# RWKV recurrence in a fused two-block kernel: the halves of a tile take turns in scores, outputs and state updates, and the states of a whole tile are multiplied in one matmul

## What is computed

```
def step(S, inp):
    r_t, w_t, k_t, v_t, a_t, b_t = inp
    sa = jnp.einsum("bhij,bhj->bhi", S, a_t)
    S = S * w_t[:, :, None, :] + sa[..., None] * b_t[:, :, None, :] + v_t[..., None] * k_t[:, :, None, :]
    y = jnp.einsum("bhij,bhj->bhi", S, r_t)
    return S, y
```

## Time and profile before

| | |
|---|---|
| median of 3 runs | 2230.68 us (2229.61 to 2230.72) |
| the profiled execution | 2232.73 us |
| its span in the profile | 2230.9 us |
| PE busy | 2089.2 us, 94% |
| DVE, ACT, POOL busy | 49%, 41%, 57% |
| mean granted PE clock | 0.962 of full speed |
| the recurrence's stretch | from about 349 to 663 us of the span |

### The profile page before, as it was taken

The page is one execution under the profiler, slowest core; times in us unless marked ns, Lnnn a source line. Parts: engine busy times, 40 slices in busy tenths (PEclk is TensorE's granted clock), DMA queues, the critical chain, the costliest instruction groups (busy, mean ns, idle before and its releaser), DMA issues.

```text
span 2230.9 us, 41267 instructions
## 1 busy us (share of the span) xinstructions
PE 2089.2 (94%) x16208; PEld 1966.6 (88%) x16208; DVE 1094.1 (49%) x1627; ACT 918.0 (41%) x1578; POOL 1278.2 (57%) x528
## 2 busy tenths in 40 slices
PE   7999898889989999999996799999998988999997
PEld 7999687878879999999895499999998877898997
DVE  5860866655555871684145467512172325324431
ACT  5333451010024434433444544444455554655552
POOL 6786350000016787788571178868675553676885
PEclk9999898999999999999997899999999998999999
DMA  6444330000014454445341045544345332343552
GB/s 261 183 173 151 114 125 27 1 1 1 1 48 161 170 183 175 157 167 186 132 151 38 20 170 175 192 163 176 144 170 191 131 114 87 139 163 142 188 189 76
DMA packets 40909, 292.06 MB, mean 131 GB/s; under 512 B 4432, under 2 KB 5712, under 8 KB 5712
## 3 DMA queue, kind: packets, MB, share of 16 engines
q1 hardware_dynamic: 40640, 289.18, 36.0%
q10 hardware_dynamic: 144, 1.05, 0.1%
HBM read 289.17 MB, written 1.05 MB: 130 GB/s over the span
## 4 chain that ended last, share of the span: by engine, by line
issue 31%; PE 30%; POOLq 18%; POOL 17%; ACT 1%; DVE 1%; DMA 0%; DVEq 0%; SPq 0%; ACTq 0%
POOLq L1827 17%; POOL w_low L1823 17%; PE ps L574 9%; PE ps L582 9%; PE ps L578 9%; PE ps L1219 1%; PE ps L1207 1%; PE ps L1197 1%; PE ps L686 0%; POOLq L1822 0%; DMA X<-x_in 0%; ACT units L1729 0%; ACT units L1284 0%; POOLq L1839 0%; DVE units L1849 0%
## 5 line engine op out<-in xcount | busy, mean ns | idle before, releaser
L1823 POOL TENSOR_TENSOR w_low<-wring,w_high 128x1024 fp32r<-128x1024 f32 x524 | 1278.0, 2454 | 931.5 <-ACT w_high L1284 902.9
L574 PE MATMUL ps<-in_high,w_high 128*128 128x256 f32 (+1 forms) x2856 | 832.2, 291 | 33.7 <-DVE in_low L1849 12.9
L582 PE MATMUL ps<-in_high,w_low 128*128 128x256 f32 (+1 forms) x2856 | 822.7, 288 | 0.0
L578 PE MATMUL ps<-in_low,w_high 128*128 128x256 f32 (+1 forms) x2856 | 820.9, 287 | 0.0
L1284 ACT ACTIVATE w_high<-wring 128x1024 fp32r<-128x1024 f32 x524 | 542.1, 1055 | 289.2 <-PE ps L574 284.8
L574 PEld LDWEIGHTS ps<-in_high,w_high 128*128 128x128 f32 x2856 | 547.7, 192 | 43.2 <-issue 37.6
L578 PEld LDWEIGHTS ps<-in_low,w_high 128*128 128x128 f32 x2856 | 547.4, 192 | 0.4
L582 PEld LDWEIGHTS ps<-in_high,w_low 128*128 128x128 f32 x2856 | 547.8, 192 | 0.0
L574 PE MATMUL ps<-hid_high,w_high 128*128 128x272 f32 (+1 forms) x880 | 255.0, 290 | 0.0
L582 PE MATMUL ps<-hid_high,w_low 128*128 128x272 f32 (+1 forms) x880 | 250.8, 285 | 0.0
L578 PE MATMUL ps<-hid_low,w_high 128*128 128x272 f32 (+1 forms) x880 | 250.6, 285 | 0.0
(11 more groups left out here) (310 smaller groups left out, 2762.1 us busy)
## 6 DMA issues: line engine op xcount, KB each, us to landing
wring<-stream SPq DMA_DIRECT2D x271, 1024.0 KB, 4.8
con<-consts SPq DMA_DIRECT2D x1, 2455.0 KB, 16.4
X<-x_in SPq DMA_DIRECT2D x1, 1088.0 KB, 7.4
units<-decay ACTq DMA_DIRECT2D x1, 1024.0 KB, 4.7
out<-AL SPq DMA_DIRECT2D x1, 1024.0 KB, 4.7
par<-params SPq DMA_DIRECT2D x1, 187.0 KB, 4.9
con<-consts SPq DMA_DIRECT2D x1, 130.0 KB, 7.3
```

Of the source, the lines that this page charges most:

```text
L574: mm = pe.matmul(o, wh, high(k), start=(k == 0), stop=False)
L578: mm = pe.matmul(o, wh, low(k), start=False, stop=False)
L582: mm = pe.matmul(o, wl, high(k), start=False, stop=(k == kt - 1))
L1823: pool.tensor_tensor(w_low[:, (half + h) % SPLIT_RING, :], wring[:, slot, h * HALF * P:(h + 1) * HALF * P], w_high[:, (half + h) % SPLIT_R ...
```

## The change

The list of heads has `u` in the outer loop, so halves take turns. `rk_update` and `rk_output` are rewritten to issue each kind of matmul for both halves before the next kind. `rk_right` multiplies the states of both halves in one matmul of 128 columns, ahead of the two others; in chunk 0, which has no state, it only has the new order.

```diff
-            rk_heads = [(2 * par + u, par, u, HD * par) for par in range(2) for u in range(2)]
+
+            rk_heads = [(2 * par + u, par, u, HD * par) for u in range(2) for par in range(2)]
...
+                z = ps[0:C, 5, 0:4 * HD].rearrange("p (a u v) -> p u a v", a=2, u=2)
                 for q, par, u, p in rk_heads:
-                    o = ps[0:C, 5, q * HD:(q + 1) * HD]
-                    mm = pe.matmul(o, rk_lk[g % 2][c][0:C, q, 0, :], rk_tm[g % 2][c][0:C, 4 + u, p:p + HD],
-                                   start=True, stop=(c == 0))
-                    if c:
-                        mm = pe.matmul(o, T0[:, 2 * g + u, t0:t0 + C], rk_s[:, c - 1, u, par, :],
-                                       start=False, stop=True)
+                    if c and par == 0:
+                        pe.matmul(z[:, u, :, :], T0[:, 2 * g + u, t0:t0 + C], rk_s[:, c - 1, u, :, :],
+                                  start=True, stop=False)
+                    mm = pe.matmul(z[:, u, par, :], rk_lk[g % 2][c][0:C, q, 0, :], rk_tm[g % 2][c][0:C, 4 + u, p:p + HD],
+                                   start=(c == 0), stop=(c == 0 or par == 1))
                 mm.then_inc(S["rk_z_ready"], 1)
...
-                for q, par, u, p in rk_heads:
-                    o = ps[p:p + HD, rk_chain_banks(g)[0], u * HD:(u + 1) * HD]
-                    pe.matmul(o, tm[0:C, u, p:p + HD], rk_sa[0:C, q, :], start=True, stop=False)
-                    mm = pe.matmul(o, tm[0:C, 2 + u, p:p + HD], tm[0:C, 4 + u, p:p + HD], start=False, stop=True)
+                for u in range(2):
+                    pair = [(2 * par + u, HD * par, ps[HD * par:HD * (par + 1), rk_chain_banks(g)[0], u * HD:(u + 1) * HD])
+                            for par in range(2)]
+                    for q, p, o in pair:
+                        pe.matmul(o, tm[0:C, u, p:p + HD], rk_sa[0:C, q, :], start=True, stop=False)
+                    for q, p, o in pair:
+                        mm = pe.matmul(o, tm[0:C, 2 + u, p:p + HD], tm[0:C, 4 + u, p:p + HD], start=False, stop=True)
                 mm.then_inc(S["rk_s_ready"], 1)
...
-                for q, par, u, p in rk_heads:
-                    o = ps[p:p + HD, rk_chain_banks(g)[1], u * P:u * P + C]
-                    pe.matmul(o, rk_sa[0:C, q, :], lb[0:C, q, 1, :], start=True, stop=False)
-                    mm = pe.matmul(o, tm[0:C, 4 + u, p:p + HD], lk[0:C, q, 1, :], start=False, stop=(c == 0))
-                    if c:
+                for u in range(2):
+                    pair = [(2 * par + u, par, HD * par, ps[HD * par:HD * (par + 1), rk_chain_banks(g)[1], u * P:u * P + C])
+                            for par in range(2)]
+                    for q, par, p, o in pair:
+                        pe.matmul(o, rk_sa[0:C, q, :], lb[0:C, q, 1, :], start=True, stop=False)
+                    for q, par, p, o in pair:
+                        mm = pe.matmul(o, tm[0:C, 4 + u, p:p + HD], lk[0:C, q, 1, :], start=False, stop=(c == 0))
+                    for q, par, p, o in pair if c else ():
                         mm = pe.matmul(o, rk_s[p:p + HD, c - 1, u, par, :], A[p:p + HD, 2 * g + u, now],
                                        start=False, stop=True)
                 mm.then_inc(S["rk_y_ready"], 1)
```

## The result

| | before | after |
|---|---|---|
| median | 2230.7 us (4 runs, 2229.6 to 2231.0) | **2202.0 us** (4 runs, 2199.2 to 2203.3) |
| ratio, 95% interval | | **0.9871** (0.9853 to 0.9888) |
| the profiled execution, its span | 2232.73, 2230.9 us | 2199.24, 2197.4 us |
| mean granted PE clock in it | 0.962 | 0.968 |

Faster by 28.7 us.

The account below looks back on a forecast made before the run. PE bounds the recurrence, DVE following closely. 15.0 + 1.0 + 1.2 + 1.6 + 3.6 = 22.4 us of PE time, less 1.4 for margins, gives 21 less: 2230.68 - 21 = 2209.7 us, range 2205 to 2218.

Parts of the forecast that it names:

- outputs (chunks 1, 2 and 0): Recurrence outputs: 8 in chunks 1 and 2 fall from 3.76 to 1.88 us, saving 15.0; chunk 0 saves 1.0.
- state updates: Recurrence state updates: second half starts at once, saving 1.2 us in chunk 1 and 1.6 us in chunk 0.
- right sides: Chunks 1 and 2: joined matmul costs what one part did, two of eight go, 0.45 us in 8 places, 3.6 us.
- scores, logits: Scores and NSA logits: alternating them gains nothing, since their halves overlap already; 24 of each costed at nothing.
- Two halves share the array: Outputs: both halves run each kind of matmul together, so two heads take about the 0.94 us of one.
- The bank of line 838: Rival, 12%: line 838's pairs, sharing one PSUM bank, go one after the other; 3.4 us back, 2213.
- The column halves: Rival, 4%: column halves don't overlap in outputs moving 128 columns; only 5.7 us gained, 2225.
- DVE takes over: Rival, 10%: DVE sets the recurrence's pace and half the gain turns into waits, 2220.
- The 1.4 us that I took off for margins: Allowance for thin DVE margins at chunk 1's outputs and the very end, taking 22.4 us down to 21.
- Slower by a price per turn: Rival, 4%: each turn between halves in updates and outputs empties the array, 0.14 us each; 13.4 us slower, 2244.
- The price of a change of tile shape: Outputs of chunks 1 and 2: each change between 128 x 64 and 64 x 64 tiles costs some 0.14 us.
- after the recurrence everything is moved up as a whole: Behind the recurrence: later work only starts earlier, its weights already waiting; `rk_o` would begin near 642 instead of 663.00 us.

Follow-up runs that it names:

- the outputs alone: Kernel before with only the outputs taking the halves in turn: 2223.5 us, ratio 0.9950 (0.9933 to 0.9967).
- the updates alone: Kernel before with only the state updates taking the halves in turn: 2240.4 us, ratio 1.0010 (0.9989 to 1.0031).

## Why the prediction was right in its steps and wrong in its number

Array time of the steps in the whole recurrence, added up from each step's start to the start of the next matmul, before and after, in the first profile of either kernel and in the second:

| step | forecast | first profiles | second profiles |
|---|---|---|---|
| outputs (chunks 1, 2 and 0) | 15.0 + 1.0 | 33.7 to 18.4, **15.3** | 34.2 to 18.2, **16.1** |
| state updates | 1.2 + 1.6 | 8.1 to 5.3, **2.8** | 7.7 to 4.8, **2.9** |
| right sides | 3.6 | 16.7 to 14.4, **2.3** | 17.1 to 13.2, **3.9** |
| the three together | 22.4 | 58.4 to 38.0, **20.4** | 59.0 to 36.1, **22.9** |
| scores, logits | 0 | 0.007 each, 0.3 in all | |

Some of these steps fell on the lower clock; the right sides of the first changed profile hold one of 2.61 us at 613 us, where the others take 1.36 to 1.39. At the full clock a right side gives 0.45, eight of them 3.6.

- **Two halves share the array** at 128 columns as at 64: right, and with it the outputs.
- **Scores and logits are worth nothing**: right, as the change of their order alone showed. They are the first part of the diff to catch the eye, and their halves ran side by side already.
- **The bank of line 838**: right to take nothing. The Trainium skill (TensorEngine Tiling (Array Packing), Gotcha 1: PSUM Pressure), by which different row tiles cannot access one bank simultaneously, would have spread 845 out; the row with four records in the time of two does not show it, for two tiles at different rows and different columns whose outputs lie on different partitions.
- **The column halves**: the rival by the rule on row groups of the Trainium skill (TensorE: Matmul & The Clock Gate, Packing small matmuls) fell; the four records of 841 have 0.24 to 0.26 us over the same 128 rows, and without changes of shape those of 841 and 843 have 0.22.
- **DVE takes over**: didn't happen. The waits before the solves are 10.6 us in both, and the margin of the earlier trace rows was met exactly. The 1.4 us that I took off for margins were lost nowhere.
- **Slower by a price per turn**: fell. With no change of shape in between, rows of four records over two halves stand 0.22 us apart, the pace of one half alone.
- **The price of a change of tile shape**, 0.14 us: right, and it was the larger part of the matter: of the 1.85 us that an output lost, its removal alone gave 1.39 in the old order. In the changed kernel 0.56 of the 1.85 are four changes fewer and the rest is overlap; without any change of shape an output takes 1.46.

**The step that failed** is the last one: "after the recurrence everything is moved up as a whole", and with it "on the median's footing 2230.68 - 21". I took the clock as a property of the kernel: the clocks of the earlier trace rows entered only as a lower bound for the saved records, by which a cut at low clock is worth 4 to 5 us more. What the runs showed in its place is that parts with equal instructions were not moved up as a whole, 10.6 us of the 33.5 in the first profiles coming after `rk_o` had begun. The granted clock varies from one execution to the next, for the same kernel by 0.958 to 0.966, which goes with 2245 to 2227 us, and the changed kernel as it stands is nearly always granted more (0.966 or more in 10 of 12 executions; the kernel before in 8 of 83). At equal mean clock, 0.966, the kernel before has 2226.7 us and the changed one about 2203.8 (5 executions): 23 less, the sum of the steps with nothing taken off. The comparison isn't clean, as a shorter phase at the lower clock is itself what a higher mean is made of; that is why it is offered as the better reading and not as a proof. The rest of the measured 28.7 to 31.6 us, 6 to 9, is by this reading clock. The 1.4 us taken off for margins are a small second part of the miss.

That `rk_o` began 22.9 us earlier, so near to the sum, was in part luck: the steps gave 20.4 us in these two profiles, and the recurrence had 41.5 us at the lower clock instead of 47.0. Over more profiles it can be told apart. From the instruction at 301.4 us to `rk_o` five profiles of kernels with the old steps have 364.2 us on the mean, 50 of them at the lower clock, and seven with the whole change 337.3 and 38: 26.9 less. Among these seven the time goes from 334.1 us with 30.0 at the lower clock to 340.4 with 44.9, 0.42 us for each microsecond. By that the 12.5 us fewer are worth 5.3 and the steps 21.6 (an estimate), as summed. Behind the recurrence the surplus lies in the first attention and at the end of the sparse attention, which takes one of three lengths (as before, some 3.5 or 5 us less) in changed and unchanged kernels alike.

The range failed for the same reason: it was made of doubts about steps, none of which came true, and had none for the ground on which the steps stand. Three runs within 1.1 us looked like a sharp figure.

**What stays open**: why this kernel meets the higher clock so regularly, in the recurrence already. The runs with idle work in `rk_o` speak for positions in time; they can say nothing of the recurrence, which lies ahead of them. Which position it is, and why the outputs alone and the updates alone rather met a lower clock (0.960), no run here tells apart.

## What to carry to other kernels

Before halves of the array are put in turns, read in the timeline whether they already overlap: the distance from one step's start to the next against the number of records at their pace. Here that told the large-looking part of the change, scores and logits (worth nothing), from the small-looking ones. Look for changes of tile shape within a step first: they cost 0.14 us each and part what would overlap, and where zeros are at hand, the larger shape costs nothing (0.22 us for a matmul of line 838 or 845 as for the others). And measure how much a kernel's own executions differ, and with what mean clock, before a forecast or a verdict of less than 1%: the same steps measured 21 us here in the runs with 1 or 2 us of idle work elsewhere, and 29 to 32 in those without.

## What the hardware showed that I had not expected

- Two 64 x 64 tiles at opposite corners write into one PSUM bank at the same time, at full pace: four records of 128 columns in 0.37 us with the 0.14 of the change of shape in it.
- Column halves that read the same 128 rows run together, each at the pace it has alone (0.22 us for a float32 matmul of 128 columns, two at once).
- The halves meet in the last two matmuls of the first half and the first two of the second, if no change of shape lies between: of six to a half two met (470.92 to 471.42), of four in an update two, of two in a score all, in either order. What in the engine makes it two, no run here tells.
- Where the lower clock falls decides the length of a stretch whose instructions are the same. From the first logit of the first attention to `at_o`: 61.1 us at a clock of 0.82, 65.3 at 0.79, 70.6 at 0.65.
- Twenty idle matmuls of 272 columns, 9.3 us, did not carry the full clock 2 us into the logits. Three more in each step held it (1.00 and 0.98) in one profile; in the other with the same matmuls the clock was 0.83 from 1183 to 1193 us and 0.68 from 1203 to 1229.
